# Expert weights computed in turns by GpSimd and VectorE, and the short path first in TensorE's program

## The chip, the cores and the metric

The kernel runs on one core of one Trainium2 chip. The metric is the device time of one execution in microseconds (us). A change of more than about 0.2% (2 us) can be told from no change here.

The engines are called as the profile calls them: PE is TensorE's matrix products, PEld its weight loads, DVE is VectorE, ACT is ScalarE, POOL is GpSimd, SP is the engine that issues the DMAs. Each runs its own program; they meet only at semaphores.

## What is computed

Two transformer layers (a gated linear recurrence, then a stick-breaking attention, each with memory attention) are followed by one block with a forgetting attention, a convolutional FFN and a gated embedding; 256 tokens, width 1024, float32. What matters here is the hierarchical mixture of experts that closes each of the first two layers. For every token one group of four is chosen by the largest group logit, then in this group the two best of its four experts; the gate of an expert is the group's probability times the softmax weight of that expert among the two, and only the product `y = sum over experts of gate * (silu(x Wg) * (x Wu)) Wd` is added. In the kernel's words:

```
g      = softmax(group logits)           # 4 per token
og     = one-hot of the best group
i4     = expert logits of that group      # 4 per token
e      = exp(i4 - max i4)
o1, o2 = one-hot of the best and of the second best of the four
gate   = e * (o1 + o2) / (1 + second best e) / (sum of exp of the group logits) / alpha
```

## The kernel before

All weights come from HBM in "halves" of 1 MB (128 x 2048 float32). SP loads a half into one of four slots of `raw`; ACT rounds it into `w_hi`; DVE subtracts to get the rest, `w_lo` (L1900, `raw` and `w_hi` both in SBUF); PE multiplies in three passes, hi x hi, hi x lo, lo x hi. A slot of `raw` is free for the next DMA when its `w_lo` is made (semaphore `lo_split`), and ACT and DVE may write a slot of `w_hi` and `w_lo` when PE has counted the old half in `half_used`. Each layer's experts take 48 halves: 4 groups of 12 (`gate_up` of four experts, two halves each, and `down`, one each). `base` is the first of them.

The order of each engine is written out by hand. In one layer's expert stage, around the change:

- DVE `mix_norm` ends with `choose_group` (semaphore `group_ready`) and `place_slots` (`placed`); ACT has `w_hi` of `base+2` by then, and DVE has `w_lo` of `base` and `base+1`.
- `gather(0)`: PE gathers the tokens of groups 0 and 1 into slots, ACT and DVE split the result into `mt_hi` and `mt_lo` (L1917, four pieces).
- DVE `weigh_experts` (L2318 to L2346): 21 small operations on the tile `rt`, each but a few waiting for the one before it. ACT adds two exponentials of 8 columns (for the groups and, after DVE's semaphore `expert_log`, for the experts), loads its table of functions and goes on to `w_hi` of `base+3`. Nothing of this is on POOL, whose whole work in this part is `rstd`, a power of one column per normalisation (L483).
- Every engine then branches on the largest group's load: over 128 tokens the dense path (a loop), otherwise the short path. With these inputs all take the short path, which is the second one in each program, so each jumps over the dense one.
- The short path on PE: `start_sums` (8 products with `ident_r`), then for each group `gate_up(0)`, `gate_up(1)`, `turn_h(0)` (L1094, transposes), `gate_up(2)`, and so on. Between the two halves of `gate_up(1)` of groups 0 and 2 stands `gates_of`: it waits for the semaphore `gated` and multiplies `perm` with the gates (8 products of 4 columns, "rt,perm" in the profile).
- The short path on DVE: four `w_lo` (`base+2` to `base+5`, `spl(6)`), then `slot_gates` (L2380: waits for `gates_of`, copies its result), then `hidden(0)` (L2392), for which `turn_h(0)` on PE waits.
- After the last group DVE normalises (`norm`, L2147 to L2167). PE meanwhile runs `keep_busy(17, 4)`: 17 products of zeros, 512 columns each, with no use but that PE isn't idle. Then `turn_block` waits for DVE's `x_res` (L2167).

Of the kernel before, what the change touches and what calls it, by code (L numbers as in the profile page):

```python
# [23 lines left out]
ALU = mybir.AluOpType  # L24
# [3 lines left out]
P = 128  # L28
# [134 lines left out]
def build(nc, a, out, FAST_LIMIT=P):  # L163
    ctx = ExitStack()
    with ctx:
# [59 lines left out]
        rt = sb("rt", [P, 228])  # L225
# [192 lines left out]

        @block.gpsimd
        def _(pool):  # L420
# [64 lines left out]

            n = 0
# [3 lines left out]
            for _ in range(6):  # L490
                for b in range(TB):
                    n += 1
                    power(n, slice(b, b + 1))

# [70 lines left out]


        r_log = rt[:, 0:40].rearrange("p (b e) -> p b e", b=2)
        r_g = rt[:, 40:48].rearrange("p (b e) -> p b e", b=2)
        r_eq = rt[:, 48:56]
        r_cum = rt[:, 56:64]  # L570
        r_og = rt[:, 64:72].rearrange("p (b e) -> p b e", b=2)
        r_t16 = rt[:, 72:104].rearrange("p (b g e) -> p b g e", b=2, g=4)
        r_e = rt[:, 104:112].rearrange("p (b e) -> p b e", b=2)
        r_o1 = rt[:, 112:120].rearrange("p (b e) -> p b e", b=2)
        r_o2 = rt[:, 120:128].rearrange("p (b e) -> p b e", b=2)
        r_m = rt[:, 128:144].rearrange("p (n b) -> p n b", b=2)
        r_g4 = rt[:, 144:152].rearrange("p (b e) -> p b e", b=2)
        r_gate = rt[:, 160:192].rearrange("p (b g e) -> p b g e", b=2, g=4)
        r_pos = rt[:, 192:204].rearrange("p (n g) -> p n g", g=4)
        r_i4 = rt[:, 208:216].rearrange("p (b e) -> p b e", b=2)  # L580
        r_e2 = rt[:, 216:224].rearrange("p (b e) -> p b e", b=2)
        r_mx = rt[:, 224:225]
# [34 lines left out]
        def _(pe):  # L617
# [337 lines left out]
            def experts(layer):  # L955
# [183 lines left out]
                with pe.If(load > FAST_LIMIT):  # L1139
# [17 lines left out]
                with pe.Else():  # L1157
                    start_sums(0)
                    start_sums(1)
                    for i in range(PAIRS):  # L1160
                        if i:
                            gather(i)
                        for q in range(2):
                            group(i, q, False)
# [8 lines left out]
            keep_busy(17, 4)  # L1173
# [110 lines left out]
            keep_busy(17, 4)  # L1284
# [609 lines left out]
        def _(dve):  # L1894
# [423 lines left out]
            def weigh_experts(layer):  # L2318

                own.link(dve.tensor_tensor(  # L2320
# [28 lines left out]
            def experts(layer):  # L2349
# [10 lines left out]
                def group(i, q, dense):  # L2360
# [347 lines left out]
```

## Time and profile before

| | us |
|---|---|
| median of 3 runs | 1001.53 (1001.23 to 1001.97) |
| the profiled execution, its own time | 1001.3 |
| its span, first to last instruction | 999.6 |
| PE busy | 966.7 (97%) |
| DVE busy | 714.7 (72%) |
| ACT busy | 549.8 (55%) |
| POOL busy | 31.3 (3%) |
| DMA, mean over the span | 206 GB/s |
| granted TensorE clock, mean | 0.999 |

The profiled execution took 1.7 us more than its span, and is within 0.3 us of the median. PE is nearly never idle, so a time is won or lost where PE has a gap, and the table cannot say where the gaps are: the timeline and the waits do. A share of 3% for POOL says that it has time for more work, not what that work costs there.

### The profile page before, as it was taken

To read this page: it belongs to the slowest core of one execution; us is meant where nothing else is said; L and a number is where in the kernel's file an instruction comes from. 1 tells how busy PE (TensorE), PEld (TensorE's weight loads), DVE (VectorE), ACT (ScalarE), POOL (GpSimd) and SP (SyncE) were. 2 spreads that over 40 slices of the span, in tenths; PEclk is the share of its full clock that TensorE was granted. 3 is DMA by queue.
4 is the path that set the end of the run, shared out by engine and by line. 5 is a ranking of instruction groups with operands and counts; after the bars stand their busy time and mean duration, and the time that the engine had idled before them with its cause. 6 is when DMAs were issued, how large, how long until landed. Compare 5 with 4: busy or idle time off the path is not lost.

```text
span 999.6 us, 15243 instructions
## 1 busy us (share of the span) xinstructions
PE 966.7 (97%) x5906; PEld 840.2 (84%) x5906; DVE 714.7 (72%) x891; ACT 549.8 (55%) x608; POOL 31.3 (3%) x73
## 2 busy tenths in 40 slices
PE   8999989999999999999999999899999999999997
PEld 8978988878888789878778888689887999998886
DVE  4788877888888774536989888845566766566566
ACT  3765644567677644653677677434553644444431
POOL 7000010000000000000000000000000000000010
PEclk9999999999999999999999999999999999999999
DMA  9653325299899945521599899736351755554611
GB/s 322 212 170 126 127 72 185 86 364 348 295 328 350 357 145 167 170 85 43 170 357 349 271 344 361 264 115 200 131 189 63 244 177 168 185 193 169 234 61 43
DMA packets 151987, 205.86 MB, mean 206 GB/s; under 512 B 6896, under 2 KB 123376, under 8 KB 151920
## 3 DMA queue, kind: packets, MB, share of 16 engines
q1 hardware_dynamic: 150912, 204.24, 60.8%
q8 instruction: 44, 0.72, 0.3%
q10 hardware_dynamic: 1008, 0.71, 0.2%
q14 instruction: 23, 0.19, 0.1%
HBM read 203.87 MB, written 1.05 MB: 205 GB/s over the span
## 4 chain that ended last, share of the span: by engine, by line
PE 73%; DVE 11%; ACT 6%; DMA 5%; issue 4%; SPq 0%; POOL 0%; ACTq 0%; POOLq 0%; DVEq 0%
PE psum L619 70%; DVE w_lo L1900 5%; ACT w_hi L1460 3%; DMA raw<-in_w_up 3%; DMA raw<-in_w_down 1%; ACT arena L1460 1%; DMA raw<-in_attn_w_in 1%; DVE stats L2147 1%; DVE x_res L2167 1%; DVE xt_lo L1917 1%; DVE mt_lo L1917 1%; ACT mt_hi L1460 0%; PE psum L1094 0%; PE psum L1345 0%; ACT L1460 0%
## 5 line engine op out<-in xcount | busy, mean ns | idle before, releaser
L1900 DVE TENSOR_TENSOR w_lo<-raw,w_hi 128x2048 fp32r<-128x2048 f32 x184 | 417.7, 2287 | 79.5 <-ACT w_hi L1460 74.5
L1460 ACT ACTIVATE w_hi<-raw 128x2048 fp32r<-128x2048 f32 (+1 forms) x186 | 353.6, 1905 | 127.5 <-PE psum L619 61.8
L619 PE MATMUL psum<-xt_hi,w_hi 128*128 128x256 f32 x704 | 200.9, 285 | 3.7 <-DVE xt_lo L1917 1.6
L619 PE MATMUL psum<-xt_hi,w_lo 128*128 128x256 f32 x704 | 199.2, 283 | 0.0
L619 PE MATMUL psum<-xt_lo,w_hi 128*128 128x256 f32 x704 | 199.1, 283 | 0.0
L619 PE MATMUL psum<-w_hi,mt_hi 128*128 128x512 f32 (+1 forms) x448 | 174.3, 389 | 2.9 <-DVE arena L2612 1.5
L619 PE MATMUL psum<-w_hi,mt_lo 128*128 128x512 f32 (+1 forms) x448 | 171.3, 382 | 0.0
L619 PE MATMUL psum<-w_lo,mt_hi 128*128 128x512 f32 (+1 forms) x448 | 171.0, 382 | 0.0
L619 PEld LDWEIGHTS psum<-xt_hi,w_hi 128*128 128x128 f32 x704 | 135.0, 192 | 5.1 <-issue 4.8
L619 PEld LDWEIGHTS psum<-xt_hi,w_lo 128*128 128x128 f32 x704 | 135.1, 192 | 0.0
L619 PEld LDWEIGHTS psum<-xt_lo,w_hi 128*128 128x128 f32 x704 | 135.0, 192 | 0.0
L619 PEld LDWEIGHTS psum<-w_hi,mt_hi 128*128 128x128 f32 x448 | 84.2, 188 | 19.6 <-DVE w_lo L1900 2.2
L619 PEld LDWEIGHTS psum<-w_hi,mt_lo 128*128 128x128 f32 x448 | 84.1, 188 | 16.8
L619 PEld LDWEIGHTS psum<-w_lo,mt_hi 128*128 128x128 f32 x448 | 84.3, 188 | 15.4
L1460 ACT ACTIVATE arena<-arena 128x512 f32<-128x512 f32 (+3 forms) x63 | 41.0, 653 | 70.3 <-DVE arena L2020 21.6
L1460 ACT ACTIVATE arena<-psum 128x256 f32<-128x256 f32 (+2 forms) x85 | 46.4, 561 | 53.9 <-PE psum L619 28.6
L619 PE MATMUL psum<-w_hi,xt_hi 128*128 128x512 f32 (+1 forms) x184 | 71.0, 386 | 4.4 <-DVE xt_lo L1917 3.0
L619 PE MATMUL psum<-w_hi,xt_lo 128*128 128x512 f32 (+1 forms) x184 | 68.4, 372 | 0.0
L619 PE MATMUL psum<-w_lo,xt_hi 128*128 128x512 f32 (+1 forms) x184 | 68.3, 371 | 0.0
L1460 ACT ACTIVATE mt_hi<-psum 128x512 fp32r<-128x512 f32 (+2 forms) x51 | 27.1, 547 | 52.9 <-PE psum L619 49.5
L619 PE MATMUL psum<-w_hi,ht_hi 128*128 128x512 f32 x128 | 52.5, 410 | 1.7 <-ACT ht_hi L1460 1.7
L1917 DVE TENSOR_TENSOR mt_lo<-psum,mt_hi 128x512 fp32r<-128x512 f32 (+2 forms) x51 | 31.2, 625 | 30.4 <-ACT mt_hi L1460 30.3
(261 smaller groups left out, 1196.6 us busy)
## 6 DMA issues: line engine op xcount, KB each, us to landing
raw<-in_w_gate SPq DMA_DIRECT2D x64, 512.0 KB, 5.1
raw<-in_w_up SPq DMA_DIRECT2D x64, 512.0 KB, 6.2
raw<-in_w_down SPq DMA_DIRECT2D x64, 512.0 KB, 5.8
raw<-in_ffn_w_up SPq DMA_DIRECT2D x44, 512.0 KB, 4.6
raw<-in_a_w_in SPq DMA_DIRECT2D x26, 512.0 KB, 6.8
raw<-in_attn_w_in SPq DMA_DIRECT2D x24, 512.0 KB, 5.2
raw<-in_ffn_w_down SPq DMA_DIRECT2D x22, 512.0 KB, 4.2
raw<-in_w_o SPq DMA_DIRECT2D x16, 512.0 KB, 4.7
```

The lines of the kernel that those rows point to most:

```text
L619: return pe.matmul(o, l, r, start=start, stop=stop, skip_group_check=skip)
L1460: return act.activation(o, i, f, **kw)
L1900: return dve.tensor_tensor(w_half(h, w_lo), w_half(h, raw), w_half(h, w_hi).bitcast(F32), ALU.subtract).then_inc(lo_split, 1)
L1917: return dve.tensor_tensor(o, whole, hi.bitcast(F32), ALU.subtract)
L2147: own.did(dve.bn_stats(stats[:, b, c, :], src))
L2167: dve.scalar_tensor_tensor(x, x, rstd[:, b:b + 1], gain[:, 1, cs], ALU.mult, ALU.add)\
```

## The change

Three things.

**The expert weights in turns.** The 21 operations of `weigh_experts` leave DVE. POOL takes the sums, differences, products and the reciprocals (as a power of -1), 16 operations per layer; DVE keeps the two picks, maximum and first one-hot, 4 operations each (`first_pick`, `second_pick`). They hand over by semaphores: `group_ready` to POOL, 3 operations, `expert_logits` to DVE, `first_pick` to POOL, 1 operation, `expert_log` to ACT (exponential), 4 operations on POOL, `others_left` to DVE, `second_pick` to POOL, 8 operations, `gated` to PE. `first_pick` stands where `weigh_experts` stood, before the branch. In the short path `second_pick` stands after the first of the four `w_lo`.

**The short path first in PE's program.** The condition is turned round (`load < FAST_LIMIT + 1`), so that PE falls through into the short path, and jumps over the dense one at its end. DVE, ACT keep their order.

**The zero products.** `keep_busy(17, 4)` behind each expert stage becomes `keep_busy(10, 4)` at the end of the short path, before the jump, and `keep_busy(2, 4)` behind it.

```diff
+            def weigh_experts(layer):
+
+                m = [r_m[:, n, :].rearrange("p (b o) -> p b o", o=1) for n in range(8)]
+                chosen = r_og.rearrange("p b (g o) -> p b g o", o=1).to_broadcast([P, 2, 4, 4])
+                pool.wait_ge(sem("group_ready"), layer + 1)
...
+                pool.tensor_tensor(r_i4, r_t16[:, :, 0, :], r_t16[:, :, 1, :], ALU.add)\
+                    .then_inc(sem("expert_logits"), 1)
+
+                pool.wait_ge(sem("first_pick"), layer + 1)
+                pool.tensor_tensor(r_e, r_i4, m[4].to_broadcast([P, 2, 4]), ALU.subtract)\
+                    .then_inc(sem("expert_log"), 1)
+                pool.wait_ge(sem("group_exp"), layer + 1)
...
+                pool.tensor_tensor(r_e2, r_e2, r_o1, ALU.subtract).then_inc(sem("others_left"), 1)
+
+                pool.wait_ge(sem("second_pick"), layer + 1)
+                one = ones[:, 0:2].rearrange("p (b o) -> p b o", o=1)
+                own.did(pool.tensor_tensor(r_o1, r_o1, r_o2, ALU.add))
+                own.link(pool.tensor_tensor(m[7], m[6], one, ALU.add))
+                own.did(pool.tensor_tensor(r_g4, r_e, r_o1, ALU.mult))
+                own.link(pool.tensor_tensor(m[7], m[7], m[2], ALU.mult))
+                own.link(pool.tensor_tensor(m[7], m[7], neg_ones[:, 0:2].rearrange("p (b o) -> p b o", o=1), ALU.pow))
+                own.link(pool.tensor_scalar(m[7], m[7], 1.0 / ALPHA, None, ALU.mult))
+                own.link(pool.tensor_tensor(r_g4, r_g4, m[7].to_broadcast([P, 2, 4]), ALU.mult))
+                own.link(pool.tensor_tensor(r_gate, r_g4.rearrange("p b (o e) -> p b o e", o=1)
+                                            .to_broadcast([P, 2, 4, 4]), chosen, ALU.mult))
+                pool.nop().then_inc(sem("gated"), 1)
...
                 gather(0)
-                with pe.If(load > FAST_LIMIT):
+                with pe.If(load < FAST_LIMIT + 1):
+                    start_sums(0)
+                    start_sums(1)
+                    for i in range(PAIRS):
...
+                    keep_busy(10, 4)
+                with pe.Else():
...
             t = SETS["L1"]
-            keep_busy(17, 4)
+            keep_busy(2, 4)
...
             t = SETS["L3"]
-            keep_busy(17, 4)
+            keep_busy(2, 4)
...
+            def first_pick(layer):
+
+                dve.wait_ge(sem("expert_logits"), layer + 1)
                 own.link(dve.tensor_reduce(r_m[:, 4, :], r_i4, AX, ALU.max))
                 first_of(r_o1, r_i4, r_m[:, 4, :])
+                dve.nop().then_inc(sem("first_pick"), 1)
+
+            def second_pick(layer):
+
+                dve.wait_ge(sem("others_left"), layer + 1)
                 own.link(dve.tensor_reduce(r_m[:, 6, :], r_e2, AX, ALU.max))
                 first_of(r_o2, r_e2, r_m[:, 6, :])
+                dve.nop().then_inc(sem("second_pick"), 1)
...
                     if q == 0 and not dense:
+                        if i == 0:
+                            spl(3)
+                            second_pick(layer)
                         spl(6)
                         slot_gates()
```

DVE's program of before, from the gather's last split to the short path's first `w_lo` (the rows in between are those of `rt` alone):

```order
L1917 TENSOR_TENSOR mt_lo<-psum,mt_hi 128x512 x4
L2320 TENSOR_TENSOR rt<-rt 128x32
L2323 TENSOR_REDUCE rt<-rt 128x8
L2324 TENSOR_REDUCE rt<-rt 128x2
L2325 TENSOR_TENSOR rt<-rt 128x8
L2215 TENSOR_TENSOR rt<-rt 128x8
L2217 SCALAR_TENSOR_TENSOR rt<-reset,rt 128x8
L2218 SCALAR_TENSOR_TENSOR rt<-rt 128x8
```

Thirteen more such rows follow before, down to the branch. In the changed program the same place, DVE ahead of the branch:

```order
L1954 TENSOR_TENSOR mt_lo<-psum,mt_hi 128x512 x4
L2358 TENSOR_REDUCE rt<-rt 128x2
L2252 TENSOR_TENSOR rt<-rt 128x8
L2254 SCALAR_TENSOR_TENSOR rt<-reset,rt 128x8
L2255 SCALAR_TENSOR_TENSOR rt<-rt 128x8
L2452 TENSOR_LOAD load_max
```

And DVE behind the branch, at the start of the short path, changed (before, the four `w_lo` stood in one row, and `slot_gate` right behind them):

```order
L1937 TENSOR_TENSOR w_lo<-raw,w_hi 128x2048
L2365 TENSOR_REDUCE rt<-rt 128x2
L2252 TENSOR_TENSOR rt<-rt 128x8
L2254 SCALAR_TENSOR_TENSOR rt<-reset,rt 128x8
L2255 SCALAR_TENSOR_TENSOR rt<-rt 128x8
L1937 TENSOR_TENSOR w_lo<-raw,w_hi 128x2048 x3
L2400 COPY slot_gate<-psum 128x8
```

So 4 of 21 operations stay ahead of the branch, 4 move between the first and the second `w_lo`, and three `w_lo` now stand behind the handover `second_pick`.

POOL's program behind that point, changed, with what each waits for (`pool_own` is POOL's own last operation). Before, POOL had only `rstd` here:

```order
L516 TENSOR_TENSOR rt<-rt 128x8 [waits first_pick]
L519 TENSOR_TENSOR rt<-rt 128x4 [waits group_exp]
L520 TENSOR_TENSOR rt<-rt 128x2 [waits pool_own]
L522 TENSOR_TENSOR rt<-rt 128x8 [waits expert_exp]
L523 TENSOR_TENSOR rt<-rt 128x8 [waits pool_own]
L527 TENSOR_TENSOR rt<-rt 128x8 [waits second_pick]
L528 TENSOR_TENSOR rt<-rt,ones 128x2
L529 TENSOR_TENSOR rt<-rt 128x8 [waits pool_own]
L530 TENSOR_TENSOR rt<-rt 128x2
L531 TENSOR_TENSOR rt<-rt,neg_ones 128x2 [waits pool_own]
L532 TENSOR_SCALAR rt<-rt 128x2 [waits pool_own]
L533 TENSOR_TENSOR rt<-rt 128x8 [waits pool_own]
```

One more, the gates themselves (128x32), ends the chain, and `gated` is given behind it. All of them read `rt` in SBUF.

PE's program at the end of the expert stage, before:

```order
L619 MATMUL psum<-mt_lo,perm_t 128x512
L1157 UNCONDITIONAL_BRANCH
L619 MATMUL psum<-zeros_r 128x512 x17
L727 MATMUL psum<-ident,x_res 128x128 x8
L619 MATMUL psum<-zeros_r 128x512 x4
```

and changed, the dense path's 630 rows now between the two groups of zero products:

```order
L655 MATMUL psum<-mt_lo,perm_t 128x512
L655 MATMUL psum<-zeros_r 128x512 x10
L1175 UNCONDITIONAL_BRANCH
L655 MATMUL psum<-xt_hi,ident_r 128x512
...
L1184 UNCONDITIONAL_BRANCH
L655 MATMUL psum<-zeros_r 128x512 x2
L763 MATMUL psum<-ident,x_res 128x128 x8
```

The jump that PE took ahead of the short path now comes behind it, between the tenth and the eleventh zero product.

## Rows read from the trace of the kernel before

**Rows 1.** The page, part 1: busy us (share of the span) xinstructions.

```profile
PE 966.7 (97%) x5906; PEld 840.2 (84%) x5906; DVE 714.7 (72%) x891; ACT 549.8 (55%) x608; POOL 31.3 (3%) x73
```

**Rows 2.** Timeline of PE, layer 0: start, us, what, [idle before <-releaser].

```profile
190.23 0.50 PE L619 MATMUL psum<-xt_hi,ident_r 128*128 128x512 f32 x1 [1.57 <-issue]
...
198.36 0.50 PE L619 MATMUL psum<-w_hi,mt_hi 128*128 128x512 f32 x1 [0.58 <-DVE w_lo L1900]
...
205.56 0.44 PE L1094 MATMUL psum<-ident,arena 128*128 128x128 f32 x2 [0.49 <-DVE arena L2392]
```

**Rows 3.** Timeline of DVE, layer 0, from the expert weights to the first gate.

```profile
190.29 0.18 DVE L2320 TENSOR_TENSOR rt<-rt 128x32 f32<-128x32 f32 x1
...
194.12 0.19 DVE L2344 TENSOR_TENSOR rt<-rt 128x32 f32<-128x32 f32 x1
196.01 8.90 DVE L1900 TENSOR_TENSOR w_lo<-raw,w_hi 128x2048 fp32r<-128x2048 f32 x4 [1.70 <-PE psum L619]
204.83 0.16 DVE L2380 COPY slot_gate<-psum 128x8 f32<-128x8 f32 x1
```

**Rows 4.** Timeline of PE, layer 1, the same stretch.

```profile
481.06 0.50 PE L619 MATMUL psum<-xt_hi,ident_r 128*128 128x512 f32 x1 [1.06 <-issue]
...
492.25 0.95 PE L619 MATMUL psum<-rt,perm 128*128 128x4 f32 x8
493.05 0.49 PE L619 MATMUL psum<-w_hi,mt_hi 128*128 128x512 f32 x1
...
496.59 0.44 PE L1094 MATMUL psum<-ident,arena 128*128 128x128 f32 x2 [0.51 <-DVE arena L2392]
```

**Rows 5.** Timeline of DVE, layer 1, the same stretch.

```profile
481.63 0.18 DVE L2320 TENSOR_TENSOR rt<-rt 128x32 f32<-128x32 f32 x1
...
487.04 8.90 DVE L1900 TENSOR_TENSOR w_lo<-raw,w_hi 128x2048 fp32r<-128x2048 f32 x4 [1.40 <-issue]
```

**Rows 6.** Timeline of POOL: two masks, a sum of 40 columns, two powers.

```profile
7.22 0.24 POOL L459 TENSOR_SCALAR_AFFINE_SELECT level_mask<-level_mask 128x64 int8<-128x64 int8 x1
...
8.07 1.10 POOL L459 TENSOR_SCALAR_AFFINE_SELECT level_mask<-level_mask 128x64 int8<-128x64 int8 x1
...
24.93 0.27 POOL L477 TENSOR_TENSOR r_sums<-arena 128x40 f32<-128x40 f32 x1
...
461.61 0.54 POOL L483 TENSOR_TENSOR rstd<-var_eps,neg_half 128x1 f32<-128x1 f32 x1 [108.45 <-DVE var_eps L2249]
467.94 1.55 POOL L483 TENSOR_TENSOR rstd<-var_eps,neg_half 128x1 f32<-128x1 f32 x1 [5.79 <-DVE var_eps L2249]
```

**Rows 7.** Timeline of DVE beside the slow ones of rows 6.

```profile
7.76 1.29 DVE L1917 TENSOR_TENSOR w_lo<-raw,w_hi 128x1024 fp32r<-128x1024 f32 x1 [1.57 <-ACT w_hi L1460]
...
467.79 1.29 DVE L2254 SCALAR_TENSOR_TENSOR x_res<-x_res,mv,gain 128x1024 f32<-128x1024 f32 x1
```

**Rows 8.** Groups by form of POOL: count | busy us, mean ns | idle before.

```profile
L483 POOL TENSOR_TENSOR rstd<-var_eps,neg_half 128x4 f32<-128x4 f32 x3 | 3.0, 1018 | 110.5 <-DVE var_eps L2112 110.5
```

**Rows 9.** Timeline of ACT, layer 0, its table load and the next half.

```profile
191.38 1.28 ACT L1694 ACT_TABLE_LOAD   x1
192.67 1.92 ACT L1460 ACTIVATE w_hi<-raw 128x2048 fp32r<-128x2048 f32 x1
```

**Rows 10.** Timeline of PE, the kernel's first products, after an idle start.

```profile
1.05 8.00 PE L619 MATMUL psum<-zeros_r 128*128 128x512 f32 x26 [1.05 <-POOL zeros_r L422]
```

**Rows 11.** Stretches behind PE's last product: span, us, PE busy (x), PEclk, DMA share, GB/s.

```profile
995.00:996.00 1.00, 0.54 (x5) 1.00 0.39 131
...
998.00:999.00 1.00, 0.00 (x0) 0.61 0.39 131
```

**Rows 12.** Timeline of PE behind the expert stage of layer 0.

```profile
346.02 4.04 PE L619 MATMUL psum<-zeros_r 128*128 128x512 f32 x17
350.37 1.23 PE L727 MATMUL psum<-ident,x_res 128*128 128x128 f32 x8 [0.32 <-DVE x_res L2167]
```

**Rows 13.** Timeline of PE, layer 1, second group's first transposes.

```profile
514.67 0.44 PE L1094 MATMUL psum<-ident,arena 128*128 128x128 f32 x2 [0.76 <-DVE arena L2392]
```

More of the change, by code:

```diff
@@ L224, in build @@
         total = sb("total", [P, 16])
-        rt = sb("rt", [P, 228])
+        rt = sb("rt", [P, 232])
         load_max = sb("load_max", [P, 1], I32)
@@ L416, in _ @@
             sp.wait_ge(out_in, 16 * len(GATE_TILES))
+        r_log = rt[:, 0:40].rearrange("p (b e) -> p b e", b=2)
+        r_g = rt[:, 40:48].rearrange("p (b e) -> p b e", b=2)
+        r_eq = rt[:, 48:56]
+        r_cum = rt[:, 56:64]
+        r_og = rt[:, 64:72].rearrange("p (b e) -> p b e", b=2)
+        r_t16 = rt[:, 72:104].rearrange("p (b g e) -> p b g e", b=2, g=4)
+        r_e = rt[:, 104:112].rearrange("p (b e) -> p b e", b=2)
+        r_o1 = rt[:, 112:120].rearrange("p (b e) -> p b e", b=2)
+        r_o2 = rt[:, 120:128].rearrange("p (b e) -> p b e", b=2)
+        r_m = rt[:, 128:144].rearrange("p (n b) -> p n b", b=2)
+        r_g4 = rt[:, 144:152].rearrange("p (b e) -> p b e", b=2)
+        r_gate = rt[:, 160:192].rearrange("p (b g e) -> p b g e", b=2, g=4)
+        r_pos = rt[:, 192:204].rearrange("p (n g) -> p n g", g=4)
+        r_i4 = rt[:, 208:216].rearrange("p (b e) -> p b e", b=2)
+        r_e2 = rt[:, 216:224].rearrange("p (b e) -> p b e", b=2)
+        r_mx = rt[:, 224:225]
+        r_w2 = rt[:, 228:232].rearrange("p (b e) -> p b e", b=2)
         @block.gpsimd
@@ L489, in _ @@
                 power(n, slice(4 * b, 4 * b + 4))
-            for _ in range(6):
+            for turn in range(6):
                 for b in range(TB):
@@ L493, in _ @@
                     power(n, slice(b, b + 1))
+                if turn in (0, 2):
+                    weigh_experts(turn // 2)
         hq = ar(0, HG_HEADS, T)
@@ L564, in turned @@
             return psum[:, 2 * b:2 * b + 2, :].rearrange("p c (k t) -> p c k t", t=P)
[L567 to L582, printed above, removed]
         MOE_SEMS = ("perm_ready", "turned_perm", "perm_out", "gathered", "xg_hi", "xg_lo", "y_sum", "y_hi",
@@ L1138, in experts @@
                 gather(0)
-                with pe.If(load > FAST_LIMIT):
+                with pe.If(load < FAST_LIMIT + 1):
+                    start_sums(0)
+                    start_sums(1)
+                    for i in range(PAIRS):
+                        if i:
+                            gather(i)
+                        for q in range(2):
+                            group(i, q, False)
+                    keep_busy(10, 4)
+                with pe.Else():
                     start_sums(0)
@@ L1156, in experts @@
                         last.then_inc(sem("moe_done"), 1)
[L1157 to L1164, printed above, removed]
             pe.wait_ge(small_l, 1)
@@ L2427, in experts @@
                 gather(0)
-                weigh_experts(layer)
+                first_pick(layer)
                 load = dve.value_load(load_max[0:1, 0:1], min_val=0, max_val=T)
+                at_branch = own.n
                 with dve.If(load > FAST_LIMIT):
+                    second_pick(layer)
+                    dve.wait_ge(sem("gated"), layer + 1)
                     for b in range(TB):
@@ L2436, in experts @@
                             group(i, q, True)
+                own.n = at_branch
                 with dve.Else():
```

29 lines of the change are left out of this document (7 added, 22 removed).

## The prediction, made before the changed kernel was run

> **What bounds the kernel now.** I read the page's busy times first: PE is busy for 97% of the span [rows 1], so the kernel is as long as PE's program plus PE's gaps, and an edit off PE is worth only the gap that it closes or opens. So I went through the timeline of PE for its gaps in the part that the change touches, and then to the engine named as releaser of each.
>
> In layer 0 there are three [rows 2]: 1.57 us ahead of the first product with `ident_r`, released by nothing (that is the branch: PE jumps over the dense path); 0.58 us at 198.36, for DVE's first `w_lo` behind the branch; 0.49 us at 205.56, where `turn_h(0)` waits for DVE's first gated hidden block. DVE shows why [rows 3]: it works on `rt` from 190.29 to 194.31, idles 1.70 us over its own branch, makes four `w_lo` without a break (8.90 us), and only then, at 204.83, copies the gates. Layer 1 is the same [rows 4, 5]: 1.06 us at the branch, 0.51 us at `turn_h(0)`. PE then works nearly without a gap to the layer's end, so what is lost or won up to `turn_h(0)` should stay in the total. **The yardstick is the start of `turn_h(0)`: 205.56 and 496.59.**
>
> **DVE ahead of the branch.** The 21 operations took 194.31 - 190.29 = 4.02 us, 0.19 us each [rows 3]. Four stay: 0.77 us. With DVE's own branch as before (1.70 and 1.40 us [rows 3, 5]) the first `w_lo` starts at 190.29 + 0.77 + 1.70 = 192.8, and in layer 1 at 481.63 + 0.77 + 1.40 = 483.8: 3.2 us earlier. It ends 2.2 us later (8.90 / 4 [rows 3]), at 195.0 and 486.0.
>
> **PE up to the gates.** PE falls through into the short path. I take the branch's 1.57 us [rows 2] as gone (between all and 1.2 us of it, since a compare and a fall-through cost something). From 190.23 to the wait at 198.36 - 0.58 = 197.78 PE works 7.55 us; starting at 188.66 it is done at 196.2, and the first `w_lo` (195.0) is there: no wait. The 12 products of the first half of `gate_up(1)` take 2.7 us (12 x 0.23; from 198.36 to 205.07 [rows 2] PE did 24 of them and the gates, 0.8 us). **PE stands at `gates_of` at 198.9.** Before, `gated` had been given at 194.3, long ahead. Now it depends on the turns.
>
> **The turns up to the second pick.** POOL's first three operations need only `group_ready`, which DVE gives before the gather, and are hidden by it. `first_pick` is given at 191.1; then POOL's subtraction, ACT's exponential, four more on POOL. POOL has no operation of 2 or 8 columns in this trace; the nearest is 0.27 us for 40 columns [rows 6], and 0.08 us more from one to the next where it waits for itself. With 0.2 to 0.35 each, `others_left` comes 1.5 to 2.1 us behind `first_pick`: 192.6 to 193.2, in DVE's branch gap or in its first `w_lo`. DVE asks for it at 195.0. Hidden; at worst its last operation is held to the end of that `w_lo`, 0.3 us. ACT gets `expert_log` some 0.4 us later than now, so table load and `w_hi` of `base+3` [rows 9] end at about 195.0, and DVE wants this half at 195.9: hidden too. `second_pick` costs DVE 0.8 us and is given at 195.9 (487.0).
>
> **The turn behind the second pick is the one that costs.** Eight operations on POOL, the last five in a chain, stand between `second_pick` and `gated`. Alone they would take 7 x 0.35 + 0.86 = 3.3 us (0.54 us for one column of power, 1.02 for four [rows 6, 8]; 0.78 for two, plus 0.08). But DVE goes straight into three `w_lo`, and the trace shows what such an operation does to POOL. The power of one column takes 0.54 us, and 1.55 us when DVE's 1.29 us operation on `x_res` and `gain`, both in SBUF, is under way [rows 6, 7]: 467.79 + 1.29 = 469.08, and POOL ends 0.41 us behind it. The mask at 8.07 takes 1.10 instead of 0.24 us; beside it runs a `w_lo` from 7.76 to 9.05, and POOL ends at 9.17. POOL's operation waits for the end of DVE's, though it reads next to nothing. So each POOL operation that meets a `w_lo` waits for its end, and POOL gets one in at each border between two of them. That is three of the eight by the end of the third `w_lo`, at 195.9 + 3 x 2.225 + 3 x 0.15 for the three let in = 203.0 (layer 1: 494.1). Then `slot_gates` makes DVE wait for PE, and five are left for POOL alone: 4 x 0.35 + 0.86 = 2.3. **`gated` at 205.3 and 496.4.** If POOL gets none in between, it is 202.6 + 3.3 = 205.9; if it gets in two at a time, 204.4.
>
> By the Trainium skill, "SBUF — State Buffer", section "Who interferes with whom", a VectorE instruction with two SBUF inputs contends with a GpSimd instruction that reads SBUF, and whichever issues second blocks fully until the first is done. By this rule the trace agrees (1.55 against 0.54 us), and the rule speaks against this change, since every `w_lo` has two SBUF inputs; without it the sum would be that of the second rival.
>
> From the start of `gates_of` to `turn_h(0)` PE needs 496.59 - 0.51 - 492.25 = 3.83 us [rows 4]. `turn_h(0)` starts at 205.3 + 3.8 = 209.1 and 500.2, against 205.56 and 496.59: **+3.6 us in each layer, +7.2.** PE idles from 198.9 to 205.3, 6.4 us.
>
> **The clock.** PE's last product of the kernel starts at 995.3; the granted clock is 1.00 until 998 and 0.61 over the next us [rows 11], so it fell from 2.4 to 1.2 GHz some 2.7 us behind the last product. An idle of 6.4 us is over twice that. What the way back costs I take from the kernel's first products: 26 of them took 8.00 us [rows 10], and 17 later ones 4.04 [rows 12], 0.2376 each; 26 x 0.2376 = 6.2, so 1.8 us were lost. +1.8 us in each layer, **+3.6**; between 0 (the clock stays) and twice that.
>
> **The zero products.** Ten take 2.4 us, 346.02 to 348.4, two more 0.5. PE needs to be ready for `turn_block` at 350.05, since it waited 0.32 us more for DVE [rows 12]. A jump as dear as the old one (1.06 to 1.57 us [rows 2, 4]), not covered at all, would end the two products at 349.9 to 350.5. PE's sequencer can go to the jump while products are queued, so I take 0; 0 to +0.4 us each. DVE's `norm` sets that point, and it isn't touched.
>
> **What is given back.** With PE 5 us later and DVE ahead of it, a gap of PE that DVE made behind `turn_h(0)` closes: 0.76 us in layer 1 [rows 13], about -0.8. In layer 0 I count nothing.
>
> **Sum.** 1001.3 + 7.2 + 3.6 - 0.8 = 1011.3; the profiled execution is 0.2 us under the median. I forecast **1011 us**.
>
> **The rivals.**
>
> 1. The chain is held, but the clock doesn't fall in one or both layers, or PE is back at once: 1001.3 + 7.2 - 0.8 = 1007.7. For it: the granted clock is 1.00 throughout the middle; against it: no gap there was over 1.7 us, so it shows nothing of a long one. Chance 0.20.
>
> 2. The other side: POOL isn't held by `w_lo`, or its operations are let in as they come. Then `gated` is given at 195.9 + 3.3 = 199.2, PE hardly waits, and DVE sets `turn_h(0)`: 4.0 us of `rt` replaced by 0.8 + 0.8, so 204.83 becomes 202.5. -2.3 us in each layer, 1001.3 - 4.6 = 996.7. It decides where `gated` falls against 205.56 - 3.83 = 201.7: earlier and the change gains, later and it loses. Two slow POOL operations of two kinds, each ending just behind DVE's, speak against it. Chance 0.12.
>
> 3. In between: POOL gets most of its chain in ahead of the second and third `w_lo` (they too would have to wait for POOL if it is first), `gated` at 201 to 203: 1000 to 1004, say 1002. For it: the first two operations behind `second_pick` start together with the second `w_lo` and may win. Against: from the third on POOL waits for itself, and DVE is at once there. Chance 0.07.
>
> 4. As forecast, and the jump behind ten zero products costs PE more than it has to spare, since it is fetched while DMA is busy with the next weights: with 3 us instead of 1.5, `turn_block` is 1.2 to 1.5 us late in each layer: 1014. Chance 0.06.
>
> **How the numbers follow.** The forecast, 1008.5 to 1014 with its bounds, has 0.55; rivals 1 to 4 have 0.20, 0.12, 0.07, 0.06. The likeliest is 1011. The range 1003 to 1016 holds the forecast, rivals 1 and 4 nearly whole and part of rival 3, some 0.8; it leaves rival 2 out. Slower by over 2 us (0.2%, about what can be told here): 0.55 + 0.20 + 0.06 + 0.03 = 0.84. Within: 0.04. Faster: rival 2, 0.12.
>
> **What would show it.** POOL's operations on `rt` behind `second_pick` take up to 2.3 us in the timeline instead of 0.2 to 0.3, and end where a `w_lo` ends; the wait of PE at the products "rt,perm" is the longest of the layer, about 6 us, released by POOL; `slot_gate` is copied at 206 instead of 204.8; the 1.57 us ahead of `ident_r` are gone; the granted clock dips behind 202; 12 zero products and a short wait stand ahead of L763. I am wrong if POOL's chain runs at 0.3 us per operation beside `w_lo` (then rival 2), or if PE's clock stays at 1.00 through the wait (rival 1).

## The result and the profile after

The changed kernel takes 1012.64 us (median of 5 runs, 1011.09 to 1014.32) against 1001.97 us before (5 runs, 1001.23 to 1002.94): 1.0106 times as long, 95% interval 1.0092 to 1.0119. The profiled execution is the slowest of the five, 1014.32 us with a span of 1012.6, 13.0 us over the span of before.

PE makes ten products fewer than before and is busy 4.7 us longer, POOL has 21 us more of busy time for 32 small operations, and one wait stands out. The page, part 1 (as [rows 1]), and the largest group of PE's waits (us in total, times, longest):

```profile
PE 971.4 (96%) x5896; PEld 844.8 (83%) x5896; DVE 710.6 (70%) x865; ACT 548.3 (54%) x608; POOL 52.3 (5%) x105
...
PE psum L655 <- POOLq L536: 11.4, 2, 5.9
```

POOL in layer 0, behind the second pick. Before the change these operations were DVE's (the end of [rows 3]):

```profile
196.65 0.21 POOL L527 TENSOR_TENSOR rt<-rt 128x8 f32<-128x8 f32 x1 [3.61 <-DVEq L2367]
196.81 2.27 POOL L528 TENSOR_TENSOR rt<-rt,ones 128x2 f32<-128x2 f32 x1
199.16 2.13 POOL L529 TENSOR_TENSOR rt<-rt 128x8 f32<-128x8 f32 x1
201.25 2.24 POOL L530 TENSOR_TENSOR rt<-rt 128x2 f32<-128x2 f32 x1
203.56 0.71 POOL L531 TENSOR_TENSOR rt<-rt,neg_ones 128x2 f32<-128x2 f32 x1
204.37 0.23 POOL L532 TENSOR_SCALAR rt<-rt 128x2 f32<-128x2 f32 x1
...
204.96 0.24 POOL L534 TENSOR_TENSOR rt<-rt 128x32 f32<-128x32 f32 x1
```

DVE in the same stretch, to be laid beside it, as [rows 3]:

```profile
196.73 6.70 DVE L1937 TENSOR_TENSOR w_lo<-raw,w_hi 128x2048 fp32r<-128x2048 f32 x3 [0.22 <-PE psum L655]
207.21 0.17 DVE L2400 COPY slot_gate<-psum 128x8 f32<-128x8 f32 x1 [3.78 <-PE psum L655]
```

Three operations on 2 or 8 columns take 2.1 to 2.3 us, each as long as one of the three `w_lo` of DVE (6.70 / 3 = 2.23). At 203.43 DVE is done, and from there the same kind of operation takes 0.20 to 0.24 us (the power 0.71). Layer 1 repeats it within a hundredth (2.27, 2.13, 2.23).

PE in both layers, as [rows 2, 4]: the wait for POOL, then `turn_h(0)`:

```profile
205.30 1.87 PE L655 MATMUL psum<-rt,perm 128*128 128x4 f32 x8 [5.88 <-POOLq L536]
...
211.81 0.38 PE L1130 MATMUL psum<-ident,arena 128*128 128x128 f32 x2
...
501.38 1.87 PE L655 MATMUL psum<-rt,perm 128*128 128x4 f32 x8 [5.55 <-POOLq L536]
...
508.30 0.38 PE L1130 MATMUL psum<-ident,arena 128*128 128x128 f32 x2
```

And the stretches around the wait of layer 0 (span, busy of PE, PEld, DVE, ACT, POOL with counts, PEclk, DMA share, GB/s), with one of layer 1 last:

```profile
201.00:203.00 2.00, 0.00 (x0) 0.00 (x0) 2.00 (x2) 1.54 (x1) 2.00 (x2) 1.00 0.96 320
203.00:205.00 2.00, 0.00 (x0) 0.00 (x0) 0.43 (x1) 0.00 (x0) 1.67 (x5) 0.85 1.07 359
205.00:207.00 2.00, 1.70 (x8) 1.70 (x9) 0.00 (x0) 0.00 (x0) 0.20 (x1) 0.50 1.10 347
...
211.00:213.00 2.00, 2.00 (x11) 1.63 (x10) 0.49 (x2) 0.99 (x3) 0.00 (x0) 0.95 0.85 254
...
498.00:498.25 0.25, 0.00 (x0) 0.00 (x0) 0.25 (x1) 0.25 (x1) 0.25 (x1) 0.50 1.03 352
```

In layer 0 PE was done at 199.4; the clock fell to 1.2 GHz at 204.4 (the 0.85 of the second row), 5.0 us later, and was back at 211.2, after 5.9 us of work at half speed. In layer 1 PE was done at 495.8, the clock was down by 498.0, 2.1 us later, and back at 508.2, after 6.8 us of work. The eight small products take 1.87 us instead of 0.95 [rows 4].

PE at the end of layer 1. The first and second rows answer to those of layer 0 in [rows 12] (the zero products, then L763). Before, the third was this row:

```profile
645.80 0.49 PE L619 MATMUL psum<-w_hi,xt_hi 128*128 128x512 f32 x1 [0.67 <-DVE xt_lo L1917]
```

and in the changed kernel (the last row is a stretch behind it, with the clock):

```profile
652.14 0.73 PE L655 MATMUL psum<-zeros_r 128*128 128x512 f32 x2 [1.02 <-issue]
653.05 1.23 PE L763 MATMUL psum<-ident,x_res 128*128 128x128 f32 x8 [0.18 <-DVE x_res L2204]
...
657.20 0.50 PE L655 MATMUL psum<-w_hi,xt_hi 128*128 128x512 f32 x1 [1.99 <-DVE xt_lo L1954]
...
658.00:660.00 2.00, 2.00 (x7) 1.54 (x6) 2.00 (x3) 0.00 (x0) 0.00 (x0) 0.59 0.02 4
```

**Where the 13.0 us of the span lie.** I laid the two timelines beside each other at fixed places. The changed execution is 0.76 us late before it comes to the change at all. Then, in layer 0, +5.49 up to `turn_h(0)` (+6.25 in all) and -0.40 to the layer's end; in layer 1, +5.86 up to `turn_h(0)` (+11.71 in all) and -1.63 to the end (+10.08 at 648.70); +1.32 by the wait ahead of `w_hi,xt_hi`; +1.6 behind it, where the clock is at 1.2 GHz again. Two things are to be explained: the 5.5 to 5.9 us in each layer, foretold in size but made of two terms that could be wrong in opposite ways, and 2.9 us at the end of layer 1 that I had not in the sum.

### The profile page after: what moved, and what is told of

Read it like the earlier page. It is cut to its first block, busy times and chain, and to the rows that moved or that the text cites. A ratio compares the mean times of both kernels' runs of the same rounds, so it can differ in the third digit from the quotient of the medians.

```text
span 1012.6 us, 15231 instructions
## 1 busy us (share of the span) xinstructions
PE 971.4 (96%) x5896; PEld 844.8 (83%) x5896; DVE 710.6 (70%) x865; ACT 548.3 (54%) x608; POOL 52.3 (5%) x105
## 4 chain that ended last, share of the span: by engine, by line
PE 73%; DVE 11%; ACT 5%; issue 4%; DMA 3%; POOL 2%; ACTq 0%; DVEq 0%; SPq 0%; POOLq 0%
PE psum L655 71%; DVE w_lo L1937 6%; ACT w_hi L1497 2%; DMA raw<-in_w_up 2%; ACT arena L1497 1%; DVE mt_lo L1954 1%; DMA raw<-in_w_down 1%; DVE xt_lo L1954 1%; PE psum L1130 1%; ACT mt_hi L1497 1%; DVE stats L2184 1%; DVE x_res L2204 0%; POOL rt L528 0%; POOL rt L530 0%; POOL rt L529 0%
## 5 line engine op out<-in xcount | busy, mean ns | idle before, releaser
L501 POOL TENSOR_TENSOR rstd<-var_eps,neg_half 128x1 f32<-128x1 f32 (+1 forms) x15 | 13.5, 907 | 894.5 <-DVE var_eps L2188 633.0
```

What stands on the lines that cost most here:

```text
L501: pool.tensor_tensor(rstd[:, cols], var_eps[:, cols], neg_half[:, cols], ALU.pow)\
```

## The experiments

### Which part of the change costs: e1_pe_part, e2_turns_only

The first is the kernel before with PE's part alone (the diff); the second the changed kernel with these lines taken back.

```diff
-                with pe.If(load > FAST_LIMIT):
+                with pe.If(load < FAST_LIMIT + 1):
+                    start_sums(0)
...
+                    keep_busy(10, 4)
+                with pe.Else():
...
-            keep_busy(17, 4)
+            keep_busy(2, 4)
```

> Only the PE part of the change on the kernel before: short path first, ten zero products at its end, two behind; the expert weights stay on DVE. Theory (the loss comes from POOL's chain): the gaps of 1.57 and 1.06 us at PE's branch close, but turn_h(0) waits for DVE, whose program is unchanged, so its start stays within 0.3 us of 205.56 and 496.59 on the scale of before, and the two gaps reappear as longer waits there. Behind each layer the jump shows as a gap of 1.0 to 1.6 us between the tenth and eleventh zero product, hidden in layer 0, up to 1.3 us and a dip of the clock (1.6 us) in layer 1: +0 to +3 us, 1002 to 1005. Rival (the order of PE's program costs the time, by code that comes late): +5 us or more, 1007 to 1012.

> Only the turns: expert weights on POOL and DVE as in the change, PE's program as before (jump ahead of the short path, 17 zero products behind). Theory: POOL's three operations behind second_pick still take 2.1 to 2.3 us each, gated comes at the same time, PE waits about 1.5 us less since it starts the short path later, turn_h(0) starts 3.6 us late with the clock at 2.4 GHz, up to 5.5 us with the clock at 1.2 GHz, in each layer; nothing is lost behind the layers: +6 to +10 us, 1008 to 1012. Rival (PE's order costs the time): within 2 us of before.

Measured: PE's part alone 1002.68 us, 1.0013 times before (1.0001 to 1.0026), 0.8 us over the 1001.86 of before that was measured with it. The turns alone 1011.32 us, 1.0102 (1.0074 to 1.0130), as much as the whole change. PE with its part alone, then with the turns alone:

```profile
198.75 0.50 PE L619 MATMUL psum<-w_hi,mt_hi 128*128 128x512 f32 x1 [2.42 <-DVE w_lo L1901]
205.95 0.44 PE L1094 MATMUL psum<-ident,arena 128*128 128x128 f32 x2 [0.51 <-DVE arena L2393]
```

```profile
204.73 1.87 PE L655 MATMUL psum<-rt,perm 128*128 128x4 f32 x8 [4.17 <-POOLq L536]
```

Alone, the short path first turns a branch gap of 1.57 us [rows 2] into a longer wait for DVE's first `w_lo` (0.58 us before, 2.42 here): DVE sets `turn_h(0)` either way. The whole loss comes with the turns.

### What holds POOL: e3_wait_gated, e6_from_psum

Two rivals to "`w_lo` holds POOL's reads": POOL is slow at such operations of itself, or beside any long DVE operation. The first kernel keeps DVE still until the gates are given; the second lets DVE run, but in layer 1 its three `w_lo` take one input from PSUM (their values are wrong by it). Both are edits of the changed kernel.

```diff
                             spl(3)
                             second_pick(layer)
+                            dve.wait_ge(sem("gated"), layer + 1)
```

The second, in layer 1, for the three halves behind the second pick:

```diff
-                            split_half(h, of_group(i, q, h + 1, PER_G))
+                                dve.tensor_tensor(w_half(h, w_lo),
+                                                  psum[:, 0:4, :].rearrange("p c n -> p (c n)"),
+                                                  w_half(h, w_hi).bitcast(F32), ALU.subtract).then_inc(lo_split, 1)
```

> The changed kernel with one more wait: DVE waits for gated behind second_pick, before the second of the four w_lo, so that no w_lo runs beside POOL's last eight operations. Theory (w_lo holds POOL): the eight take 2.5 to 3.3 us in all, none over 0.8; PE's wait at gates_of is under 1 us and the clock stays at 1.00; DVE loses those 3 us, so turn_h(0) starts 0 to 1 us later than in the kernel before: 1002 to 1006, and so 7 to 10 us faster than the change although a wait was added. Rival (POOL's operations take 2.2 us for a reason of their own, such as code or addresses): gated comes no earlier, the three w_lo start behind it, and the time rises by 4 us or more per layer, to 1020.

> The changed kernel; in layer 1 alone the three w_lo behind second_pick (halves base+3 to base+5) subtract w_hi from four banks of PSUM instead of from raw: the same engine, operation, size and output tile, but one input in SBUF instead of two. The values of these three halves are wrong by it, so the output isn't the reference's; nothing is routed behind it. Theory (what holds POOL is DVE's second input from SBUF): the three DVE operations take 2.2 us each as before, POOL's operations in layer 1 take 0.2 to 0.8, in layer 0 still 2.2; gated in layer 1 comes 3 us behind second_pick, turn_h(0) starts 7 to 8 us earlier than in the change: 1003 to 1006. Rival (any long DVE operation, or DVE's semaphores, hold POOL): no difference between the layers, 1012.6.

Measured: 1002.83 us (1.0011, 0.9999 to 1.0023) and 1004.45 us (1.0033, 1.0018 to 1.0048). POOL and DVE with the wait, layer 0:

```profile
196.61 0.20 POOL L528 TENSOR_TENSOR rt<-rt,ones 128x2 f32<-128x2 f32 x1
...
199.04 2.29 DVE L1937 TENSOR_TENSOR w_lo<-raw,w_hi 128x2048 fp32r<-128x2048 f32 x1 [2.73 <-POOLq L536]
```

and with a PSUM input, layer 1:

```profile
493.30 0.20 POOL L528 TENSOR_TENSOR rt<-rt,ones 128x2 f32<-128x2 f32 x1
493.57 0.21 POOL L529 TENSOR_TENSOR rt<-rt 128x8 f32<-128x8 f32 x1
...
493.25 6.69 DVE L2391 TENSOR_TENSOR w_lo<-psum,w_hi 128x2048 fp32r<-128x2048 f32 x3 [0.25 <-DVE rt L2255]
```

The last fence decides: the same three operations of POOL, beside DVE operations of the same length, take 0.20 us when DVE reads PSUM and SBUF, and 2.27 us in layer 0 of the same kernel, where it reads SBUF twice. Both rivals fall. It is also an answer on how the two engines share: the held POOL operations don't lengthen DVE's (6.70 us beside POOL's, 6.69 here). I wrote at the start that the engines meet only at semaphores; here DVE and POOL meet at the SBUF too, with no semaphore between them. With the wait, the chain of eight takes 2.5 us, and DVE idles 2.73 us for it, so the gain of the turns is used up.

### Wait and clock apart: e5_fill_wait

In `gates_of` of the changed kernel, PE is given something to do until the gates are there.

```diff
-                    pe.wait_ge(sem("gated"), layer + 1)
...
+                    if i == 0:
+                        keep_busy(24, 6)
+                    pe.wait_ge(sem("gated"), layer + 1)
```

> The changed kernel with 24 zero products of 512 columns (24 x 0.2376 = 5.7 us at 2.4 GHz) in PE's program ahead of its wait for the gates, in each layer: PE is busy through most of the 5.9 and 5.6 us that it now idles, and the gates are held as before. Theory (the loss in each layer has two terms, the wait of 3.6 us and the clock of 1.8 to 2.3 us): POOL's three operations still take 2.1 to 2.3 us, the wait for POOL shrinks to under 0.6 us, the granted clock stays at 1.00 from 197 to 212 and from 488 to 510, turn_h(0) starts at 209.5 and 505.5 instead of 211.8 and 508.3, and the time is 3.6 to 4.5 us under the changed kernel's: about 1008.5. Rival (the clock costs nothing by itself; the 5.5 us in each layer are all wait): the time stays at 1012.6. Rival (zero products themselves run late past the gates): over 1012.6.

Measured: 1007.34 us, 1.0050 times before (1.0036 to 1.0064), against the changed kernel's 1.0106 (1.0092 to 1.0119). More work for PE, and 5.3 us less time, more than the 3.6 to 4.5 that I had expected. PE, and a stretch of layer 0:

```profile
205.37 1.05 PE L655 MATMUL psum<-rt,perm 128*128 128x4 f32 x8 [0.43 <-POOLq L536]
...
209.15 0.38 PE L1132 MATMUL psum<-ident,arena 128*128 128x128 f32 x2
...
205.00:207.00 2.00, 1.63 (x11) 1.53 (x12) 0.50 (x2) 0.00 (x0) 0.24 (x1) 1.00 1.14 353
```

POOL is held as before (2.27, 2.14, 2.24 us) and gives the gates at the same time, but `turn_h(0)` starts at 209.15 instead of 211.81. The clock alone cost 2.66 us in layer 0. In layer 1 `turn_h(0)` is 6.13 us later than before, 3.43 of which are there at L763 already: 2.70 of wait, and 5.54 by the same two places in the changed kernel, so 2.84 of clock. **Wait 2.8 and 2.7 us, clock 2.7 and 2.8.** In layer 1 this split is good to some 0.3 us: from the start of the products with the gates to `turn_h(0)` the changed kernel takes 6.51 and 6.92 us (the fence of PE above), this one 3.78 and 3.76, which would make the clock 2.7 and 3.2.

### The same order without POOL at the end: e7_tail_on_dve, e8_tail_old_pe

The eight operations behind the second pick leave POOL and become six of DVE, and the first pick moves ahead of the gather's `w_lo`. The second kernel is the same with PE's program of before.

```diff
-                pool.wait_ge(sem("second_pick"), layer + 1)
-                own.did(pool.tensor_tensor(r_o1, r_o1, r_o2, ALU.add))
...
                             spl(3)
                             second_pick(layer)
+                            gates_here()
+            def gates_here():
+                own.link(dve.scalar_tensor_tensor(r_m[:, 7, :], r_m[:, 6, :], 1.0, r_m[:, 2, :], ALU.add, ALU.mult))
+                own.did(dve.tensor_tensor(r_o1, r_o1, r_o2, ALU.add))
+                own.link(dve.reciprocal(r_m[:, 7, :], r_m[:, 7, :]))
...
+                first_pick(layer)
                 split_to(base + START)
```

> The changed kernel, but the eight operations behind the second pick are made by DVE (six operations of 0.2 us, straight behind the second pick), POOL keeps its turns ahead of it, and the first pick stands ahead of the gather. PE's program is that of the changed kernel. Theory (only what POOL does beside w_lo is held): gates are given at about 196.5, PE doesn't wait for them, DVE is 1.2 us more ahead of its three w_lo and turn_h(0) starts at 203.5 to 204.5 and 494.5 to 495.5 instead of 205.56 and 496.59; with the stalls behind the jump (0 to 3 us) 999 to 1002 us, median 1000. Rival (DVE waits in turn for POOL, which the gather's operations hold too, so that the first pick or the second comes late): a wait of 1 to 2 us on POOL in DVE's timeline in each layer, 1002 to 1004.

> As the run before this one, with PE's program in its old order (dense path first, 17 zero products behind the layer). Theory (the order of PE's program is worth nothing where DVE sets turn_h(0), but something where PE does): PE sets turn_h(0) at 190.23 - 0 + 7.55 + 2.7 + 3.83 = 204.3, about 1.2 us earlier than before in each layer, no stall behind the layers, 999 to 1000 us; if the new order is worth its 1.57 and 1.06 us at the branch, the run before is 0.8 us ahead of this one at turn_h(0) in each layer and gives some of it back at the layers' ends.

Measured: 996.35 us, 0.9941 times before (0.9925 to 0.9956), and 998.27 us, 0.9962 (0.9949 to 0.9974). Both beat the kernel before; the first is 16 us under the changed kernel, from which it differs in who makes the last eight operations and in the place of the first pick. Better than I expected (999 to 1002). DVE and PE in layer 0 of the first, as [rows 2, 3]:

```profile
194.94 6.69 DVE L1925 TENSOR_TENSOR w_lo<-raw,w_hi 128x2048 fp32r<-128x2048 f32 x3 [0.21 <-ACT w_hi L1485]
201.55 0.16 DVE L2400 COPY slot_gate<-psum 128x8 f32<-128x8 f32 x1
...
202.28 0.44 PE L1118 MATMUL psum<-ident,arena 128*128 128x128 f32 x2 [0.26 <-DVE arena L2412]
```

`turn_h(0)` comes 3.3 us earlier than in [rows 2], 3.0 counted from the transposes of `perm` ahead of the gather. I had counted DVE's own gap at its branch (1.70 us [rows 3]) as staying; with the small operations no longer straight ahead of it, it is gone too: `mt_lo` ends at 190.51, the first `w_lo` starts at 190.65. How much of the gain is the place of the first pick and how much the last eight operations, no run separates. In the second kernel PE has its old gap back and is what is late:

```profile
191.00 0.50 PE L643 MATMUL psum<-xt_hi,ident_r 128*128 128x512 f32 x1 [1.53 <-issue]
```

and `turn_h(0)` waits for nobody at 204.78. So the short path first is worth nothing while DVE sets `turn_h(0)` (e1_pe_part), and about 1.9 us once DVE is out of the way (the two intervals just overlap), with the stalls at the other end already taken off; the next runs are about those.

### The stall behind layer 1: e4, e9, e10, e11, e12

First the obvious: seven zero products behind the jump of the changed kernel instead of two, in both layers.

```diff
-            keep_busy(2, 4)
+            keep_busy(7, 4)
```

> The changed kernel with seven zero products behind the jump at each layer's end instead of two, so 17 in all as before the change. In the changed kernel PE stalled 1.64 and 1.02 us ahead of the two products, then 1.99 us ahead of the second product of the block behind layer 1, and its clock dipped there. Theory A (the stalls are PE fetching the code behind the jump; the number of products doesn't matter to them): two stalls of 1.0 to 2.0 us ahead of the zero products stay, and turn_block comes 1.2 us (5 x 0.2376) later where DVE doesn't hold it anyway: about 1012.6 to 1014.5. Theory B (the second stall and the clock dip come of PE having been idle; more zero products behind the jump bridge them): the 1.99 us wait behind layer 1 shrinks to the 0.67 us of before and the clock stays at 1.00, about 1010.5 to 1011.5.

Measured: 1013.22 us, 1.0108 (1.0094 to 1.0122), no change. But the stall moved, which neither theory had:

```profile
656.51 1.18 PE L763 MATMUL psum<-ident,x_res 128*128 128x128 f32 x6 [3.28 <-issue]
```

Behind the jump PE had done 7 zero products and 2 of L763, nine; in the changed kernel 2 + 8 + 4 = 14. Five products more stand ahead, in layer 0, and the stall comes five earlier: as if it hung on a place in PE's code. The trace has a queue that carries code. The page of the changed kernel, part 3, and the microsecond from 654 (packets, MB, share):

```profile
q8 instruction: 44, 0.72, 0.3%
...
q8 instruction: 1, 0.02, 6.0%
```

16 KB in each packet (0.72 MB / 44). One starts at 649.6, while PE still works on its ten zero products, the next only at 654.9; it ends at 655.9, and PE goes on at 657.2. PE's part alone (e1_pe_part) shows the same stall, though PE had no long wait in it, so it doesn't come of the long idle earlier in the layer. But e6_from_psum, whose program of PE is that of the changed kernel, doesn't show it:

```profile
644.48 0.50 PE L619 MATMUL psum<-w_hi,xt_hi 128*128 128x512 f32 x1 [1.74 <-DVE xt_lo L1918]
```

```profile
648.29 0.50 PE L655 MATMUL psum<-w_hi,xt_hi 128*128 128x512 f32 x1 [0.67 <-DVE xt_lo L1954]
```

There the second packet started 4.4 us behind the first instead of 5.3, and was in by 647.1. So the place alone doesn't make a stall; the packet has to be late too, and what makes it so no run shows. To try the place, I moved the code without running any more of it: zero products at the end of layer 1's dense path, which isn't taken; five (the diff), thirty and ninety of them in e7_tail_on_dve, for e9, e10 and e11.

```diff
                         last.then_inc(sem("moe_done"), 1)
+                    if layer == 1:
+                        keep_busy(5, 4)
```

> The kernel with the gates' tail on DVE (996.35 us), and five more zero products in PE's program of layer 1, at the end of the path for over 128 tokens, which isn't taken: nothing more is executed, the code behind the jump only lies ten instructions further on. In that kernel PE stalled 1.06 us ahead of the first product behind layer 1's jump and 1.99 us ahead of the 15th, and with five more executed zero products ahead of it in layer 0 the second stall had moved from the 15th to the 10th product (3.28 us there). Theory (the second stall is PE waiting for the next piece of its own code, whose start lies at a fixed place in the program): the stall moves to the 10th product behind the jump, though nothing else is executed, and is 2 to 3.3 us long: 996.3 to 998.0. Rival (the stall comes of xt_lo of DVE or of the DMA at that time): it stays ahead of the 15th product, 1.99 us, 996.35.

> As the run before this one, with thirty unexecuted zero products (60 instructions). Theory (code comes in pieces): the border now lies ahead of the place that the jump goes to, the second stall is gone and only the wait of 0.7 us for xt_lo is left; about 1.3 us less than 996.35, 995.0, or up to 1.6 us more of stall at the jump itself as where PE fetched two pieces at once (2.59 us), then 996.5. Rival (DVE or DMA): stall of 1.99 us ahead of the 15th product, 996.35.

> As the run before this one, with ninety unexecuted zero products (180 instructions). Theory (code comes in pieces, each fetched a few us ahead where PE goes straight on): the border lies far ahead of or far behind the place that the jump goes to, so that no second stall is seen; 995.0 us, a stall of about 1 us at the jump. Rival (DVE or DMA): stall of 1.99 us ahead of the 15th product, 996.35. Rival (a longer jump costs more by itself): the stall at the jump grows over that of the run before by over 0.5 us.

Measured: 999.02 us (0.9971, 0.9958 to 0.9983), 997.29 us (0.9951, 0.9938 to 0.9965), 994.90 us (0.9939, 0.9926 to 0.9952). PE behind layer 1 without the addition, then with 5, 30 and 90:

```profile
635.93 0.73 PE L643 MATMUL psum<-zeros_r 128*128 128x512 f32 x2 [1.06 <-issue]
...
640.92 0.50 PE L643 MATMUL psum<-w_hi,xt_hi 128*128 128x512 f32 x1 [1.99 <-DVE xt_lo L1942]
```

```profile
639.19 1.12 PE L751 MATMUL psum<-ident,x_res 128*128 128x128 f32 x7 [0.41 <-DVE x_res L2194]
643.25 0.37 PE L751 MATMUL psum<-ident,x_res 128*128 128x128 f32 x1 [2.95 <-issue]
```

```profile
641.65 0.50 PE L643 MATMUL psum<-w_hi,xt_hi 128*128 128x512 f32 x1 [0.67 <-DVE xt_lo L1944]
```

```profile
638.09 0.50 PE L643 MATMUL psum<-w_hi,xt_hi 128*128 128x512 f32 x1 [0.67 <-DVE xt_lo L1944]
```

Five products that are never executed move the stall from the 15th product to the 10th (2 + 7 are done), and with thirty or ninety it isn't there. The programs of DVE and of the DMAs are the same in these kernels, so PE's wait for its own code is shown as the cause of the stall. It is longer where the border between two pieces of the code comes sooner behind the jump: in e4_seven_more, e9_five_unrun, e7_tail_on_dve and the changed kernel alike PE goes on 1.4 us behind the end of the second packet. With 2.95 us the clock fell too (0.50 from 642 to 648), and the 999.02 us are over my 998.0. The times alone show less: only the five make a kernel slower than the one without an addition (0.9958 to 0.9983 against 0.9925 to 0.9956, which just don't touch). The ninety (0.9939) can't be told from it, and the thirty (0.9951) are over it and over the 995.0 that I had expected; against the execution without an addition, the three profiled ones were 2.4 and 2.1 us late and 1.5 early ahead of the place already. By the Trainium skill, "Runtime: NRT & Kernel Launch", section "Instruction fetch mechanics", code is fetched in blocks of 16 KiB, one ahead, a taken branch out of the blocks held forces a fetch before execution goes on, and the crossing of a border is mostly hidden. The packets' size and the stall at the jump (1.06 us) agree; the border ahead of the 15th product behind the jump was not hidden, 1.99 us.

Last, ninety of them in the changed kernel itself.

> The changed kernel itself (1012.64 us; its profiled execution 1014.32) with ninety unexecuted zero products at the end of layer 1's path for over 128 tokens: it prices the one term of the change that no experiment has taken out alone. Theory (the second stall behind layer 1 and the clock that falls with it are the border between two pieces of PE's code, and the forecast's 7.2 + 3.6 - 0.8 is what the change costs without them): POOL's three operations, the waits of 5.9 and 5.6 us and the clock in both layers stay as they are, the 1.99 us behind layer 1 become 0.7 us, the clock stays at 1.00 there, and the profiled execution is 2.0 to 2.9 us under 1014.3: a median of 1010.0 to 1011.5. Rival (the stall behind layer 1 follows the long idle earlier in the layer, or is made up elsewhere): 1012.6.

Measured: 1011.09 us (4 runs, 1009.26 to 1012.40), 1.0092 (1.0075 to 1.0109), against 1.0106 (1.0092 to 1.0119): in the direction foretold, 1.5 us, but the intervals overlap, so the time alone doesn't show it. The trace does for the mechanism:

```profile
656.82 0.50 PE L655 MATMUL psum<-w_hi,xt_hi 128*128 128x512 f32 x1 [0.67 <-DVE xt_lo L1956]
...
658.00:660.00 2.00, 2.00 (x11) 1.62 (x10) 1.97 (x4) 0.00 (x0) 0.00 (x0) 1.00 0.02 4
```

The stall is gone and the clock stays at 1.00 there. In layer 1 the jump itself cost nothing here either, its twelve zero products run without a gap; in the other kernels with this order its idle was 0.6 (e6_from_psum) to 2.6 us (e5_fill_wait). This execution lost time elsewhere, ahead of the place: PE waited 1.94 us for `ht_hi` of ACT at 642.10 and ran at 1.2 GHz until 646. So 1.5 to 2.9 us is what I can say of the stall's price in the changed kernel.

## Why the prediction was right, and where it was not

The forecast of 1011 us with 1003 to 1016 is within 0.2% of 1012.64, its mechanism is the one the runs show, but each of its four terms was off by 1.2 us or more over the two layers: the wait 1.7 too much, the clock 1.9, what is given back 1.2 and the jump 2.9 too little. That the errors nearly cancelled was luck.

- **The yardstick and the way there.** Counted without the 0.76 us that the execution was late: first `w_lo` forecast for 192.8, came at 192.8; `second_pick` 195.9 and 195.8; PE at `gates_of` 198.9 and 198.7. That PE's branch gap goes was right: no gap stands ahead of the first product with `ident_r` in either layer, and in layer 1 it comes 1.24 us closer to layer 0's end than before.
- **POOL held by `w_lo`.** Right, and shown by e6_from_psum and e3_wait_gated: one operation at each border, three in all, each ending just behind DVE's. Missed by one: the first of the eight ran at once (it starts at 196.65, the `w_lo` at 196.73), so four were left at the end, not five, 1.6 us instead of 2.3. DVE lost nothing by letting them in, where I had taken 3 x 0.15. `gated` came at 204.4 instead of 205.3.
- **The wait, +3.6 in each layer.** Measured 2.8 and 2.7 (e5_fill_wait). The term was oversized by 0.8 to 0.9, for the reason just given.
- **The clock, +1.8 in each layer.** Measured 2.7 and 2.8. That it falls was right. I had priced the way back from the kernel's first products [rows 10], whose 8.00 us are only in part at 1.2 GHz. Here all that PE did for 5.9 us ran at half speed: in layer 0 eight gate products (0.9 us lost) and nine of `gate_up` at 0.43 instead of 0.23 us each (1.8 lost). Such a term is better sized by the work that stands behind the gap: half of what PE does until the clock is back.
- **The sum.** 5.4 in each layer was forecast and 5.5 and 5.9 came; the two errors, -0.9 and +0.9, cancelled. That this sum was hit says nothing of its two sizes.
- **Given back, -0.8.** It was 0.4 in layer 0 and 1.6 in layer 1.
- **Zero products and jump, 0.** This step failed, though not where rival 4 looked for it. At L763 the jump costs next to nothing, as argued. Ahead of the 15th product behind it, PE waits for the next 16 KB of its code, and in the profiled execution the clock falls behind it: +2.9 us there; by the medians of e12_after_unrun some 1.5. I had priced the jump, but not that it leaves PE without the code behind its target.
- **The rivals.** Rival 1 (no clock fall, 1007.7) was tried by e5_fill_wait: 1007.34. That the two are so near is in part luck: the rival has +6.4 over before, and that run took 5.1 more than the 1002.23 of before measured with it. Without zero products in the wait the clock did fall, in both layers. Rival 2 (POOL not held, 996.7) fell for the kernel as changed; e7_tail_on_dve, whose gates are likewise given before `w_lo`, takes 996.35, near the rival's 996.7 though by other terms (DVE's gap at the branch is gone too). Rival 4's jump was 1.6 and 1.0 us, not 3, and L763 came none the later for it in layer 1, 0.3 us in layer 0. Rival 3 had no footing: POOL waits for itself, and DVE is at once there.

## What to carry to other kernels

What work given to GpSimd costs hangs on what VectorE does in the same microseconds: where that is a run of operations with two SBUF inputs, count one GpSimd operation for each of them, even one of two columns. Six small operations that stay on VectorE (1.1 us) beat eight on GpSimd that cost 5.5 us by way of TensorE's wait and clock. Where a long wait of TensorE can't be avoided, products that only keep it busy can bring back as much as the wait itself costs; and at a taken jump in its program, look for a second stall some products behind the target. Moving the code took it away here, for a gain too small to be told in the time.

## What the runs showed of the hardware that I had not expected

- A held GpSimd operation costs VectorE nothing: three `w_lo` took 6.70 us with three GpSimd operations let in between and 6.69 with none held. The Trainium skill, "SBUF — State Buffer", section "Who interferes with whom", has the second in issue blocked until the first is done; the trace agrees for GpSimd (0.20 becomes 2.27 us).
- Small operations of GpSimd on 2 to 8 columns take 0.20 us, 0.28 from one to the next where they are linked, a power of two columns 0.71: not much dearer than DVE's (0.15 to 0.17, and 0.20 from one to the next).
- TensorE's clock went from 1.00 to 0.50 5.0 us into the wait of 5.9 us in layer 0 and 2.1 us into that of 5.6 us in layer 1, and came back only 5.9 and 6.8 us after work had begun again; the price was as large as the wait's. Shorter waits were followed by a fall too, 3.28 us in e4_seven_more, 2.95 in e9_five_unrun and 1.99 in the changed kernel; the 1.99 us of e7_tail_on_dve were not. No run here shows what decides.
- Code that is never executed changed the timeline: ninety unexecuted products took the stall of 1.99 us away; five moved it, made it 2.95, and the median 2.7 us longer.
